# Values ahead of transposes in the prompt attention, and a new order at both ends of the first stage

## The chip, the cores and the metric

One core of one Trainium2 chip. The time is device microseconds of one execution, as the median of several runs. The output must agree with the reference, all of it in float32.

## What is computed

One layer of a hybrid decoder serves a prompt of 1024 tokens and 8 samples of 4 new tokens with 8192 cached ones. Cut to what matters here:

```python
u = rmsnorm(x, attn_pre_g)
qa, kv_a, qi, ki, wi, qb, kb, vb, g_a, g_b = split(u @ w_in)          # rotary on q and k
# branch A: indexer, top 256 keys, softmax attention over these alone
score = sum_h wi[h] * relu(qi[h] . ki);  keep the top 256 admissible keys
o_a = softmax(qa . ka over the kept keys) @ va                          # 8 heads of 64, 2 groups
# branch B: differential attention, 4 heads
o_b = rmsnorm((softmax(q1 k1) - lam * softmax(q2 k2)) @ vb) * (1 - lam_init)
h += rmsnorm((sigmoid(g_a) * (o_a @ w_br_a) + sigmoid(g_b) * (o_b @ w_br_b)) @ w_out)
h += rmsnorm(swiglu(rmsnorm(h)));  h += sigmoid(h @ w_ple_gate) * (p @ w_ple_proj)
```

The outputs are h of the prompt and of the samples, and the new keys and values.

## The kernel before

The program is a row of functions, each a block in which the five engines run their own lists of instructions and meet at a barrier at the end: `project` (line 99, 0 to 438 us: projections of prompt and samples, and the samples' top-k search), `prompt_select` (887), `prompt_attend` (1121, 757 to 1025 us), `sample_select` and `sample_attend` (1818), and the tail with the dense products (2370 on).

**`prompt_attend`.** Its work is 64 units, a unit being one tile of 128 queries of one branch with one of four r: for branch A, r is a head of each of the two groups; for branch B, a head with its two maps. `UNITS` puts them in eight groups k of eight, always alternating A and B: group k takes a branch-A tile `A_TILES[k]` out of [0, 7, 1, 6, 2, 5, 3, 4] and the branch-B tile that mirrors it. A tile i has i + 1 blocks of 128 keys, so each pair has nine blocks in all; groups 0, 2, 4 and 6 have the larger unit in branch B (8, 7, 6 and 5 blocks), groups 1, 3, 5 and 7 in branch A. A unit u passes these steps, by line:

- TensorE, `scores` (1209): products into the two banks `s_bank`, of which there is one pair, so that the scores of u wait until both masks of u - 1 are done (`masked`).
- VectorE, `mask` (1368): adds the bias or the causal mask, and takes the row's extreme (`att_shift`). It moves the scores out of PSUM into `att_masked`, by m = 0 and 1, one CUSTOM_DVE instruction each.
- ScalarE, `exps` (1281): the two exponentials, m = 0 and 1.
- VectorE, `mix`: for A a reciprocal of 128x128 (1377); for B a reciprocal (1381), a weight (1383) and the difference of the two maps, `att_diff` (1388).
- TensorE, `transposes` (1225): 128x128 blocks of the probabilities (A) or of the difference (B), in groups of up to 4 into one of two banks `t_bank`. They wait for the exponentials (A) or for `att_diff` (B), and for the copy of the group before the last.
- ScalarE, `copy_group` (1291): each group of transposed blocks out of PSUM into `att_prob_t`.
- TensorE, `values` (1234 for A's scale, 1240 for A, 1243 for B): the products with the values, 2 to a block for A and 2 to a block as the profile counts them for B; they wait for the unit's last copy and for VectorE's reading of the output bank of the unit before the last.
- VectorE, `out` (1397 to 1405): reads the unit's output.

The order on each engine is written by hand, in rounds s. TensorE's round is scores(s), transposes(s - 2), values(s - 3), and, late in the stage, `turn_tile` (1251), which transposes a finished branch-B tile. ScalarE's is first exponential of s - 1, copies of the first two groups of s - 2, second exponential of s - 1, the other copies. VectorE's is mask(s), mix(s - 1), out(s - 3). SyncE only stores tiles, and GpSimd packs weights for the tail (883).

**`project`.** The prompt's tiles are taken one after the other (p = 0 is the samples' tile, the last is NTILE - 1 = 8). A tile has `begin` (transposes of its normed input, 5 groups), five chunks of `w_in`'s columns, each in four parts of 4 products of 512 columns (chunk 2 is short), and `heads` (transposes of queries and keys, 4 groups). In between, the samples' index search runs in `slots`: 64 groups of `dots`, the scores' layout, then 33 rounds of `count` and `update` (a bisection for the 256th score), `rank`, `before` and `bias`. A planner at the head of the function mixes the two lists: each slot has a weight (`BY_GROUP` 1.1, `BY_LAYOUT` 20, ...), each unit a cost (a part of a chunk 1.7, a group of heads 2.0), and `share`, the sum of costs over the sum of weights, is the budget of unit work that each slot is followed by. `late(order)` then gives TensorE's own list, in which parts of chunks are held back behind the work that others wait for; all five engines walk the same order otherwise. The prompt's rotary, the samples' sums and the counts run on VectorE (the count of one bit is line 757, 128x2052 elements; the rotary writes `pr_row`, 683), the squares and roots of the next tile's input on ScalarE (554 to 564), at the slots of the chunks.

SyncE's list is the same order: loads of x and the layer input for the tile after the next (311, issued when a `begin` slot comes), stores of `u_t`, `xp_t` and the new keys and values at the tile's slots, and at `("lay_out", 1)` the stores of the samples' scores to a DRAM buffer, a wait for all of them, and one load of 1024 KB that brings them back as `pr_flat`, laid out for counting:

```python
if slot[1]:
    sp.wait_ge(score_stored, 16 * 16)
    sp.dma_start(flat[:, 0:SPAN], score_rows.rearrange(...)).then_inc(flat_in, 16)
```

SyncE issues its DMAs in this order and into one queue; the loads of `packed` are in a queue of GpSimd's (q0).

## Time and profile before

| | us |
|---|---|
| median of 3 runs | 3039.74 (3036.61 to 3046.61) |
| the profiled execution | 3034.05 |
| its span | 3032.5 |
| TensorE busy | 2814.4 |
| VectorE busy | 1399.8 |
| GpSimd busy | 676.8 |
| ScalarE busy | 588.0 |

By stage the busy times of TensorE are 386.5 of 438 us (`project`), 315.2 of 319 (`prompt_select`), 229.6 of 268 (`prompt_attend`) and 1883 of 2007.5 (the rest); its granted clock is 0.97 to 0.99 of full in each. The profiled execution's time lies 1.5 us over its span, which is what stands around the first and last instruction. In the profile "PE" is TensorE, "PEld" its weight loads, "DVE" VectorE, "ACT" ScalarE, "POOL" GpSimd and "SP" SyncE; a bracket at the end of an instruction's row gives the time that its engine was idle before it and whose result ended that.

### The profile page before, as it was taken

To read this page: it belongs to the slowest core of one execution; us is meant where nothing else is said; L and a number is where in the kernel's file an instruction comes from. 1 tells how busy PE (TensorE), PEld (TensorE's weight loads), DVE (VectorE), ACT (ScalarE), POOL (GpSimd) and SP (SyncE) were. 2 spreads that over 40 slices of the span, in tenths; PEclk is the share of its full clock that TensorE was granted. 3 is DMA by queue.
4 is the path that set the end of the run, shared out by engine and by line. 5 is a ranking of instruction groups with operands and counts; after the bars stand their busy time and mean duration, and the time that the engine had idled before them with its cause. 6 is when DMAs were issued, how large, how long until landed. Compare 5 with 4: busy or idle time off the path is not lost.

```text
span 3032.5 us, 69638 instructions
## 1 busy us (share of the span) xinstructions
PE 2814.4 (93%) x27060; PEld 1985.4 (65%) x27060; DVE 1399.8 (46%) x2685; ACT 588.0 (19%) x1285; POOL 676.8 (22%) x1190
## 2 busy tenths in 40 slices
PE   7998979999888789999998899999889899999998
PEld 5774544666566567666766667666666666777898
DVE  2337868996678544433344443343434532102211
ACT  2441112001566310101011110011111201001101
POOL 1131003000300001134333333333424334340000
PEclk9999989999999999999999999999999999999999
DMA  7575339521600677799899998889999997673686
GB/s 229 162 203 189 90 122 324 173 71 57 216 8 12 196 223 252 267 306 342 296 338 312 322 331 288 306 297 307 311 324 326 308 311 244 215 230 122 216 268 198
DMA packets 411396, 706.03 MB, mean 233 GB/s; under 512 B 69217, under 2 KB 226017, under 8 KB 410946
## 3 DMA queue, kind: packets, MB, share of 16 engines
q1 hardware_dynamic: 325298, 467.93, 47.0%
q0 software_dynamic: 75456, 232.86, 22.8%
q8 instruction: 215, 3.52, 0.5%
q10 hardware_dynamic: 10320, 0.84, 0.3%
q14 instruction: 107, 0.88, 0.1%
HBM read 659.40 MB, written 90.00 MB: 247 GB/s over the span
## 4 chain that ended last, share of the span: by engine, by line
PE 52%; DMA 4%; issue 3%; DVE 2%; SPq 2%; ACT 2%; DVEq 1%; POOLq 1%; POOL 0%; ACTq 0%
PE sa_t L1685 39%; PE sa_s L2041 4%; PE sa_o L2104 3%; DMA sa_ring_va<-cache_a_kv 2%; PE sa_s L2051 1%; DMA tw_w<-packed 1%; PE sa_stat L2081 1%; DMA early_w<-packed 1%; PE sa_o L2108 1%; ACT sa_prob_t L2182 1%; DVEq L1768 1%; SPq L1996 1%; POOLq L1982 1%; DVE tw_rstd L1760 1%; SPq L1995 0%
## 5 line engine op out<-in xcount | busy, mean ns | idle before, releaser
L1983 POOL DMA_DIRECT2D sa_ring_v<-cache_b_kv x512 | 275.4, 538 | 1097.0 <-PE sa_o L2108 753.3
L2221 DVE STREAM_TRANSPOSE sa_key_b<-sa_ring_k 128x2048 f32<-128x2048 f32 x128 | 295.0, 2307 | 261.6 <-PE sa_s L2041 217.7
L1685 PE MATMUL sa_t<-tw_z,early_w 128*128 128x304 f32 (+1 forms) x1664 | 392.4, 391 | 2.3 <-DVE tw_z L1771 1.4
L1685 PE MATMUL sa_t<-tw_z,tw_w 128*128 128x304 f32 (+1 forms) x1664 | 393.4, 392 | 0.8 <-DVE tw_sig L1774 0.8
L1685 PEld LDWEIGHTS sa_t<-tw_z,early_w 128*128 128x128 f32 x1664 | 285.8, 191 | 93.3 <-issue 19.6
L1685 PEld LDWEIGHTS sa_t<-tw_z,tw_w 128*128 128x128 f32 x1664 | 285.7, 191 | 90.6 <-issue 16.0
L1984 POOL DMA_DIRECT2D sa_ring_va<-cache_a_kv x512 | 274.4, 536 | 53.9 <-issue 27.4
L485 PE MATMUL pr_acc<-pr_w,pr_u_t 128*128 128x512 f32 (+1 forms) x640 | 255.6, 544 | 0.0
L1012 PE MATMUL sel_g<-sel_u,sel_gw 128*128 128x352 f32 x768 | 227.5, 459 | 0.0
L1012 PEld LDWEIGHTS sel_g<-sel_u,sel_gw 128*128 128x128 f32 x768 | 145.8, 190 | 81.9 <-issue 0.8
L2041 PE MATMUL sa_s<-sa_key_b,sa_q_pad 32*32 32x256 f32 x8192 | 183.6, 398 | 4.0 <-issue 4.0
L485 PEld LDWEIGHTS pr_acc<-pr_w,pr_u_t 128*128 128x128 f32 x640 | 109.6, 194 | 94.2 <-issue 94.1
L2104 PE MATMUL sa_o<-sa_ring_v,sa_prob_t 128*8 128x128 f32 x4096 | 139.0, 277 | 25.1 <-DMA sa_ring_va<-cache_a_kv 24.6
L2041 PEld LDWEIGHTS sa_s<-sa_key_b,sa_q_pad 32*32 32x32 f32 x8192 | 119.2, 105 | 56.2 <-issue 26.3
L2104 PEld LDWEIGHTS sa_o<-sa_ring_v,sa_prob_t 128*8 128x8 f32 x4096 | 100.2, 90 | 77.5 <-issue 46.0
L1720 ACT ACTIVATE tw_sig<-sa_t 128x304 f32<-128x304 f32 (+1 forms) x88 | 34.4, 391 | 559.9 <-PE sa_t L1685 559.9
L1685 PE MATMUL sa_t<-early_o,early_w 128*128 128x304 f32 (+1 forms) x512 | 126.1, 400 | 12.5 <-DMA early_w<-packed 4.7
L1701 ACT ACTIVATE tw_sq<-sa_t 128x304 f32<-128x304 f32 (+1 forms) x64 | 25.0, 391 | 511.9 <-PE sa_t L1685 511.9
L1774 DVE TENSOR_TENSOR tw_sig<-sa_t,tw_sig 128x304 f32<-128x304 f32 (+1 forms) x88 | 37.4, 425 | 183.9 <-ACT tw_sig L1720 183.4
L1685 PE MATMUL sa_t<-early_o,tw_w 128*128 128x304 f32 (+1 forms) x512 | 120.7, 390 | 0.8 <-DMA tw_w<-packed 0.7
L1685 PEld LDWEIGHTS sa_t<-early_o,early_w 128*128 128x128 f32 x512 | 89.6, 195 | 41.2 <-issue 16.3
L1685 PE MATMUL sa_t<-tw_x,tw_w 128*128 128x304 f32 (+1 forms) x448 | 106.7, 392 | 1.0 <-DMA tw_w<-packed 1.0
(347 smaller groups left out, 3758.4 us busy)
## 6 DMA issues: line engine op xcount, KB each, us to landing
sa_ring_k<-cache_b_kv SPq DMA_DIRECT2D x512, 256.0 KB, 5.7
sa_ring_v<-cache_b_kv POOLq DMA_DIRECT2D x512, 256.0 KB, 6.2
early_w<-packed SPq DMA_DIRECT2D x168, 512.0 KB, 5.2
tw_w<-packed SPq DMA_DIRECT2D x168, 512.0 KB, 5.9
sa_ring_ka<-cache_a_kv SPq DMA_DIRECT2D x512, 64.0 KB, 5.8
sa_ring_va<-cache_a_kv POOLq DMA_DIRECT2D x512, 64.0 KB, 6.1
packed<-w_gate_up POOLq DMA_DIRECT2D x44, 512.0 KB, 14.7
gate_t<-sel_gate SPq DMA_DIRECT2D x16, 528.0 KB, 3.0
```

Of the source, the lines that this page charges most:

```text
L485: ins = pe.matmul(acc[m % ACC][:, 0:hi - lo], u_t[:, p % 2, k, :], w[:, k, lo:hi], start=(k == 0), stop=(k == KC - 1))
L1012: ins = pe.matmul(g_bank[n % 4][:, 0:PIECE], gw[j % GATE_W][:, k, :], u[:, k, c * PIECE:(c + 1) * PIECE], start=(k == 0), stop=(k == KC - 1))
L1685: ins = pe.matmul(out, self.w[at % self.SLOTS][:, first + k - lo, :], src[:, cols], start=(k == 0), stop=(k == depth - 1))
L1720: nc.scalar.activation(self.sig[:, n % 2, cols], read, ACT.Sigmoid).then_inc(self.sig_set, 1)
L1760: nc.vector.reciprocal(rstd, rstd)
L1768: dve.drain()
L1774: nc.vector.tensor_tensor(sig[:, n % 2], bank, sig[:, n % 2], ALU.mult).then_inc(self.freed_by(g), 1)
L1983: pool.dma_start(ring_v[:, n % RING, :], rows_of(cache_b, page, 1)).then_inc(v_in[n // 4 % 2], 16)
L1984: pool.dma_start(ring_va[:, n % RING, :], rows_of(cache_a, page, 1)).then_inc(va_in[n // 4 % 2], 16)
L2041: ins = pe.matmul(s_bank[32 * h:32 * h + 32, k, 0:CH * 32], q_pad[rows, d, h, 24 - 8 * j:56 - 8 * j], key_b[rows, :, 4 * h + d, :], start= ...
L2104: pe.matmul(o_bank[32 * h:32 * h + 8, 0:P], prob_t[:, g, 0, at:at + 8], ring_v[:, g, h * P:(h + 1) * P], start=False, stop=False, tile_pos ...
L2221: nc.vector.transpose(key_b[:, at:at + 4].rearrange("p g n s -> p (g n s)"), ring_k[:, at:at + 4, :].rearrange("p g e -> p (g e)")).then_i ...
```

## The change

The diff makes two independent edits.

In `prompt_attend`, TensorE's round becomes scores(s), values(s - 3), transposes(s - 2). Nothing else in that function changes.

In `project`, the load of `pr_flat` with its wait becomes a slot of its own, `("lay_in",)`, behind `("lay_out", 1)`. The layout's weight of 20 is split into 8 for the store and 12 for the load, so that the planner puts units between them; the weight of the bias goes from 16 to 22, and `share` falls from 0.854 to 0.836. In the last tile, the group of heads 1 goes from behind chunk 3 to behind chunk 4. By the planner's code, this is what it comes to:

- SyncE: the load of x (512 KB) and of the layer input (128 KB) for tile 5, the store of `u_t` (512 KB) and the store of `xp_t` (640 KB) stand ahead of the wait and of the load of `pr_flat`, and stood behind them.
- TensorE: count 0 stands ahead of the four groups of heads of tile 3, and stood behind them. At the end, the sum of the last count stands ahead of chunk 8 1 2, and stood behind chunk 8 2 0 (chunk p c part); the second group of heads of tile 8 goes behind chunk 8 4.
- VectorE and ScalarE follow the same order; the counts in between are grouped slightly otherwise among the same units.

```diff
--- before.py
+++ after.py
@@ -114,7 +114,7 @@
     chunks = [(0, 512), (512, 1024), (1024, 1092), (1092, 1604), (1604, 2116)]
     pair_cols = [C_QA + P * j for j in range(4)] + [C_KA] + [C_QI, C_QI + P] + [C_KI] + \
                 [C_QB + P * j for j in range(4)] + [C_KB + P * j for j in range(4)]
-    BY_GROUP, BY_LAYOUT, BY_COUNT, BY_RANK, BY_BIAS = 1.1, 20.0, 5.2, 6.0, 16.0
+    BY_GROUP, BY_STORE, BY_LOAD, BY_COUNT, BY_RANK, BY_BIAS = 1.1, 8.0, 12.0, 5.2, 6.0, 22.0
 
     def begin(p):
         return [[("begin", p, g) for g in range(5)]] if p < NTILE else []
@@ -141,16 +141,16 @@
     for p in range(2, NTILE - 1):
         units += chunk(p, 0) + turn_heads(p - 1) + chunk(p, 1) + chunk(p, 2) + chunk(p, 3) + begin(p + 1) + chunk(p, 4)
     last = [[slot] for slot in turn_heads(NTILE - 1)[0]]
-    units += chunk(NTILE - 1, 0) + turn_heads(NTILE - 2) + chunk(NTILE - 1, 1) + chunk(NTILE - 1, 2) + last[0:1] + chunk(NTILE - 1, 3) + last[1:2]
-    units += chunk(NTILE - 1, 4) + last[2:4]
+    units += chunk(NTILE - 1, 0) + turn_heads(NTILE - 2) + chunk(NTILE - 1, 1) + chunk(NTILE - 1, 2) + last[0:1] + chunk(NTILE - 1, 3)
+    units += chunk(NTILE - 1, 4) + last[1:4]
 
     slots = [("small",), ("turn", 0)]
     for n in range(GROUPS):
         slots += [("turn", n + 1)] if n + 1 < GROUPS else []
         slots += [("dots", n)] + {11: [("new_store",)], 27: [("new_load",)], 53: [("lay_out", 0)]}.get(n, [])
-    slots += [("lay_out", 1)]
+    slots += [("lay_out", 1), ("lay_in",)]
     slots += [(kind, i) for i in range(COUNTS) for kind in ("count", "update")] + [("rank",), ("before",), ("bias",)]
-    weights = {"dots": BY_GROUP, "lay_out": BY_LAYOUT, "count": BY_COUNT, "rank": BY_RANK, "bias": BY_BIAS}
+    weights = {"dots": BY_GROUP, "lay_out": BY_STORE, "lay_in": BY_LOAD, "count": BY_COUNT, "rank": BY_RANK, "bias": BY_BIAS}
     share = sum(cost_of(u) for u in units) / sum(weights.get(s[0], 0.0) for s in slots if s != ("lay_out", 0))
     order, budget, spent, g = [s for u in first for s in u], 0.0, 0.0, 0
     for slot in slots:
@@ -415,9 +415,9 @@
                             at = c * 64 + s * 16
                             sp.dma_start(score_rows[s, c, lo * NQ:hi * NQ].rearrange("q p s -> p q s"),
                                          score[at:at + 16, lo * NQ:hi * NQ, :]).then_inc(score_stored, 16)
-                    if slot[1]:
-                        sp.wait_ge(score_stored, 16 * 16)
-                        sp.dma_start(flat[:, 0:SPAN], score_rows.rearrange("j c q p s -> (j c q) (p s)")).then_inc(flat_in, 16)
+                elif slot[0] == "lay_in":
+                    sp.wait_ge(score_stored, 16 * 16)
+                    sp.dma_start(flat[:, 0:SPAN], score_rows.rearrange("j c q p s -> (j c q) (p s)")).then_inc(flat_in, 16)
                 elif slot[0] == "bias":
                     sp.wait_ge(bias_ready, 1)
                     sp.dma_start(a["new_bias"].rearrange("c q s -> (c q) s"), hit[(SLICES - 1) * QS:P, SPAN:FLAT]).then_inc(nb_stored, 16)
@@ -1256,10 +1256,10 @@
                         scores(s)
                     if s < 2:
                         repeat_product(pe, t_bank[0][:, 0, :], ident[:], (3, 9)[s])
+                    if s >= 3:
+                        values(s - 3)
                     if 2 <= s < U + 2:
                         transposes(s - 2)
-                    if s >= 3:
-                        values(s - 3)
                     if 0 <= s - ROOT - 1 < LAST:
                         turn_tile(s - ROOT - 1)
                 repeat_product(pe, s_bank[0][:, 0:P], ident[:], 10)
```

## Rows read from the trace of the kernel before


**Rows 1.** Busy time by engine: PE, PEld, DVE, ACT, POOL; then clock, DMA share, GB/s

```profile
757.00:1025.00 268.00, 229.63 (x1820) 162.06 (x1821) 201.19 (x582) 168.69 (x415) 29.37 (x37) 0.97 0.26 80
```

**Rows 2.** The chain that ended last, prompt attention's end: start, us, what

```profile
1024.83 0.26 SPq L2006
```

**Rows 3.** Waits in the prompt attention: total us, times, longest

```profile
ACT att_prob_t L1291 <- PE att_t L1225: 79.9, 56, 2.8
...
PE att_t L1225 <- DVE att_diff L1388: 11.3, 15, 1.3
...
PE att_t L1225 <- ACT att_prob_t L1291: 9.5, 16, 2.2
```

**Rows 4.** Timeline, first group: start, us, engine, instruction [idle before <- releaser]

```profile
780.70 0.49 PE L1209 MATMUL att_s<-keep_ka,keep_qa 64*128 64x128 f32 x4 [1.28 <-DVE att_shift L1368]
...
781.12 0.44 PE L1225 MATMUL att_t<-keep_ident,att_prob 128*128 128x128 f32 x2
...
781.39 1.95 PE L1243 MATMUL att_o<-keep_vb,att_prob_t 128*128 128x128 f32 x16
...
781.54 0.43 ACT L1291 COPY att_prob_t<-att_t 128x128 f32<-128x128 f32 x2 [0.47 <-PE att_t L1225]
...
781.86 1.16 ACT L1281 ACTIVATE att_prob<-att_masked,att_shift 128x1024 f32<-128x1024 f32 x1
...
783.14 0.17 DVE L1381 RECIPROCAL att_inverse<-att_total 128x2 f32<-128x2 f32 x1 [0.64 <-ACT att_prob L1281]
...
785.67 1.23 DVE L1368 CUSTOM_DVE_ANT_0 att_masked<-att_s,keep_causal 128x1024 f32<-128x1024 f32 x1
...
788.11 1.99 PE L1209 MATMUL att_s<-keep_ka,keep_qa 64*128 64x512 f32 x8 [1.23 <-DVE att_shift L1368]
```

**Rows 5.** Timeline of TensorE, groups 2 and 6 of the prompt attention

```profile
844.61 0.70 PE L1209 MATMUL att_s<-keep_ka,keep_qa 64*128 64x256 f32 x4 [0.97 <-DVE att_shift L1368]
...
845.74 1.73 PE L1243 MATMUL att_o<-keep_vb,att_prob_t 128*128 128x128 f32 x14
...
967.06 1.28 PE L1243 MATMUL att_o<-keep_vb,att_prob_t 128*128 128x128 f32 x10
```

**Rows 6.** Timeline, second group, the large unit in branch A

```profile
811.26 0.49 PE L1209 MATMUL att_s<-keep_kb,keep_qb 64*128 64x128 f32 x4
...
819.09 0.49 PE L1209 MATMUL att_s<-keep_kb,keep_qb 64*128 64x128 f32 x4
...
820.09 0.39 PE L1234 MATMUL att_o<-keep_ident,att_inverse_of 128*128 128x128 f32 x2
...
822.04 0.95 DVE L1377 RECIPROCAL att_inverse_of<-att_total 128x128 f32<-128x128 f32 x1 [0.96 <-ACT att_prob L1281]
...
822.31 0.70 PE L1209 MATMUL att_s<-keep_ka,keep_qa 64*128 64x256 f32 x4
...
823.43 0.42 DVE L1368 CUSTOM_DVE_ANT_0 att_masked<-att_s,keep_bias 128x256 f32<-128x256 f32 x1
```

**Rows 7.** First stage: timelines, DMA share in 0.75 us slices (216:246), issue, busy times

```profile
220.38 13.90 PE L485 MATMUL pr_acc<-pr_w,pr_u_t 128*128 128x512 f32 x32
...
231.31 0.36 SPq L311 DMA_DIRECT2D pr_x<-x_all  x1
...
236.14 2.35 DVE L757 TENSOR_SCALAR_CACHE_REDUCE pr_hit<-pr_flat,pr_edge 128x2052 f32<-128x2052 f32 x1 [6.41 <-DMA pr_flat<-score_rows]
...
240.83 1.94 PE L447 MATMUL pr_turn<-pr_ident,pr_row 128*128 128x128 f32 x8 [5.68 <-ACT pr_heads L564]
...
DMA  9999999999998632100009799999999999999999
...
xp_t<-pr_xp_t SPq DMA_DIRECT2D x1, 640.0 KB, 30.4
...
240.00:246.00 6.00, 5.17 (x14) 3.52 (x15) 2.73 (x5) 2.45 (x8) 3.23 (x4) 0.52 1.06 338
...
420.07 1.11 PE L447 MATMUL pr_turn<-pr_ident,pr_row 128*128 128x128 f32 x4 [8.06 <-DVE pr_row L683]
```

## The prediction

> **What bounds the kernel now.** I read the busy times by stage first, then the chain of waits, then the timelines of the two stages that the diff touches. The program has four stretches between barriers of all engines: the first stage, the prompt's selection, the prompt attention (757 to 1025 us) [rows 1], and the rest. The chain that ended last begins at 1024.8, at the first instruction behind the barrier that closes the prompt attention [rows 2]. So what the first stage or the prompt attention gains or loses moves the end by the same amount; nothing later absorbs it.
>
> In the prompt attention TensorE is the busiest engine (229.6 of 268 us), but it is not full, and neither is VectorE (201) or ScalarE (169). ScalarE waits 79.9 us for TensorE's transposes, in 56 waits; TensorE waits 11.3 us for VectorE's `att_diff` and 9.5 us for ScalarE's copies [rows 3]. Such a picture is a ring of dependences, and the question is which instructions are in the ring.
>
> The timeline shows one pair of units in the first group of tiles, a small unit of branch A (1 block) and a large one of branch B (8 blocks) [rows 4]. Each row starts when the one before it in the ring ends. VectorE ends masking the large unit; TensorE, which had waited 1.28 us for that, makes the small scores at 780.70 and the small transposes at 781.12; ScalarE, which had waited 0.47 us for them, copies at 781.54 and only then runs the second exponential of the large unit, at 781.86 (line 1281 stands behind line 1291 in its order); VectorE waited 0.64 us for it, starts the reciprocal at 783.14, then the mix, and masks the next large unit from 785.67 to 788.0; TensorE's next scores start at 788.11. The period is 788.11 - 780.70 = 7.41 us, and every piece of it is in the ring. The 16 products of the large unit's values (781.39, 1.95 us) are **outside** it: they run after the transposes, beside ScalarE's and VectorE's work.
>
> **The change, prompt attention.** The swap puts those values between the scores and the transposes. The transposes then start one block of values later, so do the copy, the second exponential, the mix, the mask and the next scores. ScalarE's 0.47 us is a wait for these very transposes, so it is no slack. For this group a pair costs 7.41 + 1.88 = 9.3 us (1.95 us less the overlap of the last product). By the same reading the large branch-B units of the other groups put in 14 products in 1.73 us, 12 (between the two), and 10 in 1.28 us [rows 5], so 1.6, 1.4 and 1.2 us; there too the ring has no slack, as TensorE itself waits for the mask ahead of the small scores (0.97 us in the first of them).
>
> With a large unit of branch A the round is bound by TensorE instead, and the ring has room [rows 6]: small scores at 819.09, as soon as the mask is done, scale and values from 820.09 to the next scores at 822.31 (2.22 us), reciprocal at 822.04, next mask at 823.43. The ring is 4.3 us up to that mask, plus two masks of 1024 columns (785.67 to 788.0 [rows 4], 2.3 us) = 6.6, against a period of 7.8. With 2.2 us put in, less 0.35 us for which the small transposes now wait for `att_diff`, it is 8.5, against a period that the same work made 7.8: some 0.8 us more a pair. The same sum gives 0.9, 0.8 and 0.2 us for the other three such groups.
>
> There are 4 pairs in each of the 8 groups: 4 x (1.88 + 1.6 + 1.4 + 1.2) = 24.3 and 4 x (0.8 + 0.9 + 0.8 + 0.2) = 10.8, together 35 us. At the seven borders between groups two large or two small units meet, where I count half of it; that takes about 5 us off. The waits of TensorE for `att_diff` do go, since the values fill them, but TensorE is then in front of a later wait for the mask. I take **+30 us**. Bounds: below, only the branch-B groups pay, for three of their four pairs each and at 2/3: +12; above, all of the 35 and a lower clock (below): +50.
>
> **The change, first stage.** With the new weights and list the planner's code gives this order. What SyncE issues: x and the layer input of tile 5 (640 KB), then the stores of `u_t` (512 KB) and `xp_t` (640 KB), now go ahead of the wait for the stored scores and of the 1024 KB load of `flat`. What TensorE runs: count 0 now stands ahead of the four groups of heads of tile 3, where it stood behind them.
>
> The stall that this aims at is plain: TensorE ended tile 4's first chunk at 234.28, did two groups of transposes and then waited 5.68 us, until 240.83, for ScalarE [rows 7], which sat in front of the square of tile 5's x; that load was issued only behind `flat`, at 231.31. With x issued some 9 us earlier this wait goes. Next is what is late then: TensorE reaches count 0 at 234.3, and count 0 needs `flat`, which landed at 236.14, plus 2.35 us of counting, so TensorE stands until some 238.9 (236.14 + 2.35, and the rest of the count, estimated at 0.4; 4.6 us), and only then makes 16 transposes, of which it made 8 before. By 243 it has done the same work as before. The swap of waits alone is worth nothing, 0 us.
>
> `flat` itself is issued behind 1.8 MB of the same queue. The spread: at the 338 GB/s of the stretch behind it [rows 7] these are 5.3 us, of which the idle time of the DMA engines from 228.7 to 231 (slices 18 to 20 of rows 7's line of 40) may hide some or nothing; the `xp_t` store took 30.4 us to land when GpSimd's packing was in flight, which would make `flat` some 20 us late. I take +4, near the former: most of the stores' way lies in the idle time, and the packing resumes only at 232. The ends are 0 and +20, and the latter is a rival below. Behind the waiting count on VectorE stand the rotary of tile 4's first chunk and all other counts; TensorE waits for them.
>
> After the transposes of the heads the clock matters: from 240 to 246 us TensorE had a granted clock of 0.52, its level of 1.2 GHz, after the stall, and 8 transposes took 1.94 us [rows 7]. I take the same cost for either order. The Trainium skill, TensorE: Matmul & The Clock Gate, Part 4: PE-mode transpose, says that transposes do not count as busy time for the clock; by that the clock would come back only behind the products that follow, and the first stage would lose some 1.5 us more, since twice the transposes now come first. The rows fit either reading.
>
> At the end of the stage the work goes the other way. TensorE waited 8.06 us at 420.07 for the rotary of the last tile's second chunk, which VectorE does behind the bias [rows 7]. Now the last count stands earlier in TensorE's list: two parts of chunk 1 and one of the short chunk 2 of the last tile lie behind it instead of ahead (8 instructions of 13.90 / 32 = 0.43 us [rows 7] and 4 short ones, some 4 us) and fill the wait, and the heads that waited go behind chunk 4. I take -5; the bounds are 0 and the wait itself, -8. The counts between hold the same work on both engines in another grouping: 0, from -2 to +3, one count of 2.35 us out of step either way.
>
> **Sum.** Profiled execution 3034.05 us, + 30 + 4 - 5 = 3063. That execution lies 5.7 us below the median of the three runs, 3039.74; on the median's scale the forecast is 3069 us. About 0.3% (9 us) is what a measurement of this kernel tells from no change.
>
> **The rivals.**
> (1) TensorE is the bound, and filling its waits pays. Then its 11.3 us for `att_diff` and some of the 9.5 us for copies go, and with -1 of the first stage the time is 3039.74 - 17 = 3023. This needs ScalarE's second exponential to have slack behind the small transposes. It decides the sign: the ring must have more than the block's 1.2 to 2.2 us to spare; [rows 4] show none, [rows 6] show 1.1. Chance 0.07. [...]
> (2) The clock. With the longer rounds TensorE's share falls from 86% to 77%; at 86% the granted clock of the stage was 0.97 [rows 1], so it fell now and then. If a third of the stage were at the low level, the small scores and the block in the ring would cost twice as much: about +15 more, 3084. Chance 0.14.
> (3) `flat` is stuck behind the stores: +16 beyond the 4, 3085. Chance 0.06.
> (4) The rings overlap and half of the loss is absorbed: +15 in place of +30, 3054. Chance 0.11.
> (5) The loss is small and meets the gain of the first stage's end: 3042. Chance 0.05; that the order does not change is excluded, as the lists differ.
> The forecast itself has 0.57, and its own range is 3059 to 3079. The range 3047 to 3091 takes in (2), (3), (4) and the bounds, and leaves (1) and (5) out. Slower by over 0.3%: 0.57 + 0.14 + 0.06 + 0.11 = 0.88; within: 0.05; faster: 0.07.
>
> **What would show it.** In the profile after: the prompt attention is near 298 us where it was 268; in its first pairs the scores of small units are 9.3 us apart; TensorE's wait for `att_diff` falls below 3 us while its wait for `att_shift` (the mask) grows to some 30 or more, and ScalarE's for transposes grows beyond 100. In the first stage: the 5.68 us wait is gone and one of about 5 to 9 us stands ahead of count 0, with `flat` landing 0 to 8 us later; the 8.06 us wait shrinks to 4 or less. The prediction is wrong if the second exponential of a large unit does not start later against the mask before it.

## The result, and the profile after

The changed kernel takes 3069.77 us (median of 4 executions, 3065.26 to 3072.98); the kernel before, timed beside it, 3038.35 us. The ratio is 1.0105, with a 95% interval of 1.009 to 1.0121: the change makes the kernel about 31 us slower. The forecast was 3069 us, with a range of 3047 to 3091.

The busy times by stage of the kernel after (columns as in [rows 1]; the borders are this kernel's own barriers):

```profile
0.00:434.00 434.00, 387.10 (x2053) 245.23 (x2055) 236.92 (x515) 114.00 (x256) 60.92 (x77) 0.98 0.54 163
...
753.50:1053.90 300.40, 243.54 (x1820) 166.51 (x1820) 200.71 (x581) 168.64 (x415) 29.20 (x36) 0.96 0.24 72
1053.90:3068.90 2015.00, 1890.57 (x22197) 1399.78 (x22197) 694.32 (x910) 255.24 (x514) 550.67 (x1029) 0.97 0.83 279
```

The first stage ends at 433.8 us where it ended at 438.4. The prompt attention, 753.5 to 1053.9, takes 300.4 us where the kernel before took 266.9 (757.9 to 1024.8, both from TensorE's first scores to the first load behind the barrier) [rows 2], with the same instructions in it: VectorE is busy for 200.7 us and ScalarE for 168.6, as before, and TensorE for 243.5 where it was 229.6. The rest takes 2015.0 us against 2007.7. That last difference is not the change's: over the profiles of all the kernels below, none of which differs there, the rest takes between 2002.9 and 2017.6 us. So between the two profiled executions (3070.48 and 3034.05 us) the sum is -4.6 + 33.5 + 7.3, plus 0.2 in the stage between, and between the medians some 31.

The waits in the prompt attention, of the kernel after, over the whole of that stage (total us, times, longest; the kernel before's, over its whole stage, are those of [rows 3]):

```profile
ACT att_prob_t L1291 <- PE att_t L1225: 117.9, 60, 5.5
...
DVE att_inverse L1381 <- ACT att_prob L1281: 35.8, 22, 3.8
...
PE att_s L1209 <- DVE att_shift L1368: 29.7, 30, 1.9
...
PE att_t L1225 <- DVE att_diff L1388: 8.9, 11, 2.2
```

ScalarE's wait for transposes grew from 79.9 to 117.9 us and TensorE's wait for the mask (`att_shift`), which was 10.3 us, to 29.7. TensorE's wait for `att_diff` fell from 11.3 to 8.9 only. VectorE now waits 35.8 us for the second exponential ahead of the reciprocal, from 16.8.

One pair of units in the first group, timeline of the kernel after, which answers to [rows 4]:

```profile
767.64 0.49 PE L1209 MATMUL att_s<-keep_ka,keep_qa 64*128 64x128 f32 x4 [1.20 <-DVE att_shift L1368]
...
768.06 2.05 PE L1243 MATMUL att_o<-keep_vb,att_prob_t 128*128 128x128 f32 x16
...
769.95 0.38 PE L1225 MATMUL att_t<-keep_ident,att_prob 128*128 128x128 f32 x2
...
770.31 0.43 ACT L1291 COPY att_prob_t<-att_t 128x128 f32<-128x128 f32 x2 [1.68 <-PE att_t L1225]
770.63 1.16 ACT L1281 ACTIVATE att_prob<-att_masked,att_shift 128x1024 f32<-128x1024 f32 x1
...
771.91 0.17 DVE L1381 RECIPROCAL att_inverse<-att_total 128x2 f32<-128x2 f32 x1 [2.42 <-ACT att_prob L1281]
...
774.44 1.23 DVE L1368 CUSTOM_DVE_ANT_0 att_masked<-att_s,keep_causal 128x1024 f32<-128x1024 f32 x1
...
776.88 0.49 PE L1209 MATMUL att_s<-keep_ka,keep_qa 64*128 64x128 f32 x4 [1.94 <-DVE att_shift L1368]
```

The rows are the ring, in its order: small scores at 767.64, now the 16 products of the large unit's values for 2.05 us, and only then the two small transposes at 769.95; ScalarE waited 1.68 us for them (0.47 before), copies, and starts the second exponential at 770.63, 2.99 us behind the scores where it was 1.16 us behind (780.70 to 781.86 in [rows 4]); VectorE waited 2.42 us for it (0.64), masks from 774.44, and TensorE's next scores start at 776.88, 9.24 us after the last ones. Before it was 7.41.

The first stage, timeline of the kernel after, which answers to [rows 7]:

```profile
217.33 13.90 PE L485 MATMUL pr_acc<-pr_w,pr_u_t 128*128 128x512 f32 x32
...
218.82 0.36 SPq L311 DMA_DIRECT2D pr_x<-x_all  x1
...
225.11 1.62 SPq L420 DMA_DIRECT2D pr_flat<-score_rows  x1
...
234.43 2.35 DVE L757 TENSOR_SCALAR_CACHE_REDUCE pr_hit<-pr_flat,pr_edge 128x2052 f32<-128x2052 f32 x1 [7.75 <-DMA pr_flat<-score_rows]
...
237.07 0.59 PE L543 MATMUL pr_once<-pr_count,pr_same 128*128 128x1 f32 x2 [5.85 <-DVE pr_flipped L759]
...
237.52 3.91 PE L447 MATMUL pr_turn<-pr_ident,pr_row 128*128 128x128 f32 x16
...
413.89 9.87 PE L485 MATMUL pr_acc<-pr_w,pr_u_t 128*128 128x512 f32 x16 [3.69 <-DVE pr_row L683]
```

The 5.68 us wait for ScalarE is gone, and one of 5.85 us ahead of the sum of count 0 (L543) stands in its place. All 16 transposes of the heads come behind it. At the end, the wait for the last tile's rotary has shrunk from 8.06 to 3.69 us; it now stands ahead of products (L485), as the heads that waited have moved behind them.

### The profile page after: what moved, and what is told of

Read it like the earlier page. It is cut to its first block, busy times and chain, and to the rows that moved or that the text cites. A ratio compares the mean times of both kernels' runs of the same rounds, so it can differ in the third digit from the quotient of the medians.

```text
span 3068.9 us, 69638 instructions
## 1 busy us (share of the span) xinstructions
PE 2836.5 (92%) x27060; PEld 1995.9 (65%) x27060; DVE 1399.4 (46%) x2685; ACT 587.4 (19%) x1285; POOL 676.4 (22%) x1190
## 4 chain that ended last, share of the span: by engine, by line
PE 52%; DMA 4%; issue 3%; DVE 2%; ACT 2%; SPq 1%; POOLq 1%; DVEq 1%; POOL 0%; ACTq 0%
PE sa_t L1685 39%; PE sa_s L2041 4%; PE sa_o L2104 4%; DMA sa_ring_va<-cache_a_kv 2%; PE sa_s L2051 1%; PE sa_stat L2081 1%; DMA tw_w<-packed 1%; PE sa_o L2108 1%; ACT sa_prob_t L2182 1%; DMA early_w<-packed 1%; POOLq L1982 1%; PE sa_t L1655 1%; DVE tw_rstd L1760 0%; DVEq L1768 0%; DMA y<-tw_y_row 0%
## 5 line engine op out<-in xcount | busy, mean ns | idle before, releaser
L485 PE MATMUL pr_acc<-pr_w,pr_u_t 128*128 128x512 f32 (+1 forms) x640 | 254.4, 543 | 3.7 <-DVE pr_row L683 3.7
L485 PEld LDWEIGHTS pr_acc<-pr_w,pr_u_t 128*128 128x128 f32 x640 | 109.0, 194 | 97.9 <-issue 93.3
L1685 PE MATMUL sa_t<-early_o,early_w 128*128 128x304 f32 (+1 forms) x512 | 123.4, 394 | 11.8 <-DMA early_w<-packed 6.0
L1685 PEld LDWEIGHTS sa_t<-early_o,tw_w 128*128 128x128 f32 x512 | 87.5, 190 | 30.2 <-issue 7.6
```

The lines of the kernel that those rows point to most:

```text
L485: ins = pe.matmul(acc[m % ACC][:, 0:hi - lo], u_t[:, p % 2, k, :], w[:, k, lo:hi], start=(k == 0), stop=(k == KC - 1))
L1685: ins = pe.matmul(out, self.w[at % self.SLOTS][:, first + k - lo, :], src[:, cols], start=(k == 0), stop=(k == depth - 1))
```

## Experiments

All times are beside runs of the kernel before on the same chip. "Pair" is the time from one reciprocal of a branch-A unit (line 1377 of the kernel before) to the next, one pair of units; "attention" is from the first scores to the first load behind the barrier, and "first stage" the start of the next stage's first product, each of the profiled execution.

| kernel | ratio to before (95%) | first stage ends | attention |
|---|---|---|---|
| before | 1 | 438.4 | 266.9 |
| after | 1.0105 (1.009 to 1.0121) | 433.8 | 300.4 |
| attn_only | 1.0138 (1.012 to 1.0156) | 436.2 | 303.1 |
| first_only | 0.9986 (0.9977 to 0.9995) | 433.8 | 267.0 |
| exps_after | 0.998 (0.9967 to 0.9993) | 436.4 | 261.6 |
| exps_before | 0.9964 (0.995 to 0.9977) | 437.4 | 256.8 |
| swap_large_turn | 1.0019 (1.0009 to 1.003) | 439.7 | 269.7 |
| swap_small_turn | 1.0132 (1.0115 to 1.0149) | 438.5 | 303.4 |
| exps_first | 0.996 (0.9946 to 0.9974) | 432.5 | 256.9 |
| exps_large | 0.9956 (0.9941 to 0.997) | 438.4 | 254.4 |
| exps_large_ahead | 0.9958 (0.9939 to 0.9976) | 439.6 | 252.9 |
| exps_large_first | 0.9945 (0.9928 to 0.9962) | 436.5 | 254.8 |
| first_load | 0.9994 (0.9979 to 1.0008) | 443.0 | 265.4 |
| first_end | 0.9966 (0.995 to 0.9983) | 432.7 | 263.2 |

**The two edits apart.** attn_only is the kernel before with

```diff
-                    if 2 <= s < U + 2:
-                        transposes(s - 2)
                     if s >= 3:
                         values(s - 3)
+                    if 2 <= s < U + 2:
+                        transposes(s - 2)
```

> Only the swap in the prompt attention, the first stage as before. Theory (a ring of scores, transposes, copy, second exponential, mix and mask takes in the values): the prompt attention takes 300 us as in the changed kernel, 33.5 us more than before, and the whole 3072 us. Rival (part of the loss of the whole change comes from the first stage, through when transfers and packing reach the attention): the attention takes 285 us or less, the whole under 3060.

Measured: the attention takes 303.1 us, the whole 3074.65 against 3036.55. The loss belongs to the swap alone; the rival falls.

first_only is the changed kernel with that swap taken back.

> Only the new order of the first stage, the attention as before. In the changed kernel the first stage is 4.6 us shorter, of which 3.0 us were already there before the stored scores are loaded, where only a stall of 2.6 us near 184 us is missing. If the gain is the end of the stage alone: 3038.4 - 2 to - 4, some 3035 us. If the missing stall belongs to the new order too: 3038.4 - 5, some 3033 us. If the stage after the attention, which took 7.3 us longer in the changed kernel's profile, is slower because of the first stage: 3040 us or more.

Measured: 3031.74 against 3036.55 us, a gain of 4 us give or take 3. The attention's pairs are those of the kernel before (7.41 and 7.42 us in the first group), so the first stage's new order does not reach them. The rest of this profiled execution took 2017.6 us, the longest of all; but the 11 timed runs lie lower (this profile's 3039.5 is their highest), so that rest is no part of the change.

**The ring cut on ScalarE.** exps_after is the changed kernel, and exps_before the kernel before, with

```diff
                     if s - 1 < U:
                         exps(s - 1, 0)
+                        exps(s - 1, 1)
                     if 2 <= s < U + 2:
                         for g in range(min(2, len(groups[s - 2]))):
                             copy_group(s - 2, g)
-                    if s - 1 < U:
-                        exps(s - 1, 1)
```

> The changed kernel, with both exponentials of a unit ahead of the copies on ScalarE instead of the copies of the first two groups between them. Theory (the values delay the small transposes, these the copy, and the copy the second exponential, which stands behind it in ScalarE's list): the ring is cut there, the attention falls from 300 to some 275 us, the whole to 3045. Rival (the loss comes from the lower granted clock in the attention, or from TensorE having too much to do): the cut changes little, attention 295 us or more, the whole 3063 or more.

> The kernel before, with both exponentials of a unit ahead of the copies. Theory: the ring is shorter by the small copy (0.32 us) and ScalarE's wait (0.47 us) in the groups whose large unit is in branch B, and the copies of large units come later, which TensorE's transposes into two banks wait for: attention 262 to 270 us (267 before), the whole 3034 to 3042. Rival (the copies are what TensorE needs first): attention above 275, the whole above 3047.

Measured: exps_after 3029.68 us, attention 261.6; exps_before 3023.33 us, attention 256.8. Nothing was changed on TensorE, and 39 us of attention went between the changed kernel and exps_after, 10 us between the kernel before and exps_before. The same pair as above, timeline of exps_after (its lines behind 1281 stand one line higher):

```profile
776.84 0.49 PE L1209 MATMUL att_s<-keep_ka,keep_qa 64*128 64x128 f32 x4 [0.79 <-DVE att_shift L1367]
...
777.26 2.05 PE L1243 MATMUL att_o<-keep_vb,att_prob_t 128*128 128x128 f32 x16
...
777.80 1.15 ACT L1281 ACTIVATE att_prob<-att_masked,att_shift 128x1024 f32<-128x1024 f32 x1
...
779.15 0.38 PE L1225 MATMUL att_t<-keep_ident,att_prob 128*128 128x128 f32 x2
...
779.51 0.43 ACT L1291 COPY att_prob_t<-att_t 128x128 f32<-128x128 f32 x2 [0.47 <-PE att_t L1225]
...
781.62 1.23 DVE L1367 CUSTOM_DVE_ANT_0 att_masked<-att_s,keep_causal 128x1024 f32<-128x1024 f32 x1
...
784.05 1.13 PE L1209 MATMUL att_s<-keep_ka,keep_qa 64*128 64x512 f32 x4 [0.79 <-DVE att_shift L1367]
```

The values still stand ahead of the small transposes, the copy is still late at 779.51, but the second exponential already starts at 777.80, as soon as the first ends; the next scores come 7.21 us after these. With TensorE's old order (exps_before) the pair is 7.17: in this pair the swap costs 0.04 us where it costs 1.8 with the ring closed. Over the whole attention it still costs 4.8 us (261.6 against 256.8), so the loss is gone but for a seventh; 1.3 us of the rest stand in the first pair behind the first group (9.34 against 8.04), and where the others come from was not followed up. Both forecasts were too careful: the theory said 275 and 262 to 270 us. The ring had bound the kernel before as well. Its waits in exps_before say so (total us, times, longest):

```profile
ACT att_prob_t L1291 <- PE att_t L1225: 64.4, 61, 3.4
...
PE att_s L1209 <- DVE att_shift L1367: 8.5, 16, 1.0
...
DVE att_inverse L1380 <- ACT att_prob L1281: 1.0, 1, 1.0
```

VectorE's wait for the exponential ahead of the reciprocal (L1380 here) is 1.0 us, where it was 16.8.

**Which half of the swap.** swap_large_turn and swap_small_turn are the kernel before with the swap in half of the rounds:

```diff
+                    ahead = s >= 3 and (s - 2 >= U or blocks_of(s - 2) > blocks_of(s - 3))
+                    if ahead:
+                        values(s - 3)
                     if 2 <= s < U + 2:
                         transposes(s - 2)
-                    if s >= 3:
+                    if s >= 3 and not ahead:
                         values(s - 3)
```

and with `<` for `>` in the second.

> The kernel before, with the values ahead of the transposes only in the rounds where the unit to be transposed is the larger of the two, so that a small unit's values (0.8 to 1.5 us) go ahead of a large unit's transposes. Theory: the copy of a large unit is not what its neighbour's second exponential waits for, and these transposes stood waiting for the difference anyway, so the small values fill that wait: attention 263 to 268 us (267 before), the whole 3033 to 3038. Rival (any values ahead of any transposes cost their own length): these hold about 3 tenths of the swapped products, attention 275 to 278 us, the whole 3046.

> The complement: the values ahead of the transposes only in the rounds where the unit to be transposed is the smaller, so that a large unit's values (1.3 to 2.2 us) go ahead of a small unit's transposes. Theory: this half holds the whole loss, attention 299 to 304 us, the whole 3070 to 3075. Rival (each swapped block costs its own length): attention 290 to 293 us, the whole 3061.

Measured: with a small unit's values ahead of a large unit's transposes, attention 269.7 us and the whole 0.2% slower; with a large unit's values ahead of a small unit's transposes, 303.4 us and 1.3% slower. The second half holds the whole loss and the rival falls, since it had put 3 tenths on the other. The first half was not as harmless as I expected: +2.8 us, not -4 to +1, though TensorE's wait for `att_diff` fell from 11.3 to 4.1 us. In the first group its pairs are 7.62 and 7.45 us (7.42 and 7.41 before); in the fourth to the seventh some are longer by 0.5 to 0.7 us (7.84, 8.09, 7.87 and 8.15). Why is open. The whole, 3043.0 us, also missed its forecast of 3033 to 3038. Timeline of TensorE in swap_small_turn, first group:

```profile
773.36 0.49 PE L1209 MATMUL att_s<-keep_ka,keep_qa 64*128 64x128 f32 x4 [0.60 <-DVE att_shift L1371]
...
782.60 0.49 PE L1209 MATMUL att_s<-keep_ka,keep_qa 64*128 64x128 f32 x4 [1.35 <-DVE att_shift L1371]
...
783.02 2.05 PE L1243 MATMUL att_o<-keep_vb,att_prob_t 128*128 128x128 f32 x16
```

The period is 9.24 us, as in the changed kernel (767.64 to 776.88), and so is the next one, where the changed kernel's has 10.60 (see the clock, below).

**The first stage, part by part.** first_load keeps the bias's weight of 16 and the last heads' old place, and takes only the load slot; first_end takes only those two and leaves the layout in one piece:

```diff
first_load
-    BY_GROUP, BY_LAYOUT, BY_COUNT, BY_RANK, BY_BIAS = 1.1, 20.0, 5.2, 6.0, 16.0
+    BY_GROUP, BY_STORE, BY_LOAD, BY_COUNT, BY_RANK, BY_BIAS = 1.1, 8.0, 12.0, 5.2, 6.0, 16.0
...
-    slots += [("lay_out", 1)]
+    slots += [("lay_out", 1), ("lay_in",)]
first_end
-    BY_GROUP, BY_LAYOUT, BY_COUNT, BY_RANK, BY_BIAS = 1.1, 20.0, 5.2, 6.0, 16.0
+    BY_GROUP, BY_LAYOUT, BY_COUNT, BY_RANK, BY_BIAS = 1.1, 20.0, 5.2, 6.0, 22.0
...
-    ... + chunk(NTILE - 1, 3) + last[1:2]
-    units += chunk(NTILE - 1, 4) + last[2:4]
+    ... + chunk(NTILE - 1, 3)
+    units += chunk(NTILE - 1, 4) + last[1:4]
```

> The kernel before with only the layout split into a store and a load slot (weights 8 and 12), the bias's weight and the last heads as before. Theory (this part exchanges TensorE's wait for the square of tile 5's x against one for count 0, and delays the load a little): from the transposes of tile 5's x to the end of the four groups of heads 25.5 us where the old order takes 23.6 (mean of three profiles), the wait of 8.06 us near 420 stays, the first stage ends some 2 us later, the whole +2 us. Rival (removing the 5 us wait pays by itself): the stage ends 2 us or more earlier.

> The complement: the bias's weight 22 and the last heads' new place, the layout in one slot as before. Theory: the wait ahead of the last tile's heads shrinks from 8.06 to some 3.7 us, and the 1.69 us wait near 186 us goes, as these come from the weight and not from the load's place: the first stage ends 4 to 5 us earlier, at 432 to 434 us, the whole -4 us. Rival (they come from the load's place): both waits stay.

Measured: first_load 0.9994, no difference that counts; first_end 0.9966, that is 10 us faster, with an interval of 5 to 15. In its profile the first stage ends 5.7 us earlier, and the attention, whose code is that of the kernel before, is 3.7 us shorter, most of it by the clock (see below); what of the 10 us is the change's is open. Timelines of first_load and of first_end:

```profile
233.08 1.97 SPq L420 DMA_DIRECT2D pr_flat<-score_rows  x1
...
245.25 0.59 PE L543 MATMUL pr_once<-pr_count,pr_same 128*128 128x1 f32 x2 [5.38 <-DVE pr_flipped L759]
...
424.51 1.12 PE L447 MATMUL pr_turn<-pr_ident,pr_row 128*128 128x128 f32 x4 [8.06 <-DVE pr_row L683]
```

```profile
227.60 0.34 SPq L420 DMA_DIRECT2D pr_flat<-score_rows  x1
...
232.73 2.35 DVE L757 TENSOR_SCALAR_CACHE_REDUCE pr_hit<-pr_flat,pr_edge 128x2052 f32<-128x2052 f32 x1 [3.43 <-DMA pr_flat<-score_rows]
...
235.37 0.38 PE L543 MATMUL pr_once<-pr_count,pr_same 128*128 128x1 f32 x2 [1.53 <-DVE pr_flipped L759]
...
238.46 1.94 PE L447 MATMUL pr_turn<-pr_ident,pr_row 128*128 128x128 f32 x8 [1.77 <-ACT pr_heads L564]
...
413.11 9.92 PE L485 MATMUL pr_acc<-pr_w,pr_u_t 128*128 128x512 f32 x16 [3.69 <-DVE pr_row L683]
```

The gain of the first stage belongs to first_end, whose wait near 413 us is 3.69 us and which has none of the 1.69 us wait near 186 that the old weights have in all eight profiles. The early wait can only come from the bias's weight, since the last heads stand 200 us behind it; which of the two shrinks the late one was not separated. first_load keeps the 8.06 us wait. There I was wrong in a detail: in first_load TensorE's heads still stand ahead of count 0, so it is the weight of the bias, through `share`, that moves count 0 ahead of them, and not the load's slot (the planner's code gives the same order). Nor was the path as long as forecast: from the transposes of tile 5's x to the first product behind the heads and count 0 it is 23.9 us, where I had said 25.5, and 21.9 us in first_end. In first_end `flat` is issued ahead of x, lands 5.1 us later (227.60 to 232.73), and the two waits that follow are 1.53 and 1.77 us. With the load slot as well (the changed kernel) `flat` takes 9.3 us (225.11 to 234.43), and the wait is 5.85. From TensorE's transposes of tile 5's x to the end of the stage it is 218.7 us in the mean of seven profiles of the old order, 216.6 in five of the whole new one, 221.2 in first_load and 214.5 in first_end. By the means the load slot costs 2 to 2.5 us and the rest gains 4. But the five profiles of the new order fall into two kinds, 213.8 and 213.9 us against 218.1 to 218.9, and the clock parts them. The 16 products behind the 3.69 us wait take 7.13 us in the first two and 9.75 to 9.96 us in the other three, and in first_end. Timeline of first_only, to be held against the last rows of the two timelines of the kernel after and of first_end:

```profile
416.80 7.13 PE L485 MATMUL pr_acc<-pr_w,pr_u_t 128*128 128x512 f32 x16 [3.70 <-DVE pr_row L683]
```

At the same clock there, the load slot costs 3.9 us (218.4 against 214.5). With one profile of first_end and one of first_load, 2 to 4 us is as close as it can be put.

**Versions that beat both.** exps_first adds the new first stage to exps_before; exps_large adds to exps_before the half of the swap that had cost little (small values ahead of large transposes); exps_large_first has all three; exps_large_ahead is the kernel before with the second exponential ahead only where its unit is the larger one:

```diff
+                    ahead = s - 1 < U and s >= 2 and blocks_of(s - 1) > blocks_of(s - 2)
                     if s - 1 < U:
                         exps(s - 1, 0)
+                    if ahead:
+                        exps(s - 1, 1)
                     if 2 <= s < U + 2:
                         for g in range(min(2, len(groups[s - 2]))):
                             copy_group(s - 2, g)
-                    if s - 1 < U:
+                    if s - 1 < U and not ahead:
                         exps(s - 1, 1)
```

> TensorE's order of the attention as before, both exponentials ahead of the copies on ScalarE, and the new first stage: the two that gained alone. Additive: 3023 - 4 = 3019 us, the attention at 257. Rival (the gains overlap, or the rest of the program takes the first stage's gain back): 3023 or more.

> Both exponentials ahead of the copies, the first stage as before, and the small units' values ahead of the large units' transposes. With the ring cut TensorE (230 us busy of 257) is nearer to being what bounds, so filling its waits for the difference (some 6 us) could pay: attention 252 to 257 us, the whole 3019 to 3023. Rival (the large transposes and their copies now end the round, so the small values ahead of them cost their length in part): attention 260 to 264 us, the whole 3027 to 3031.

> The kernel before, with the second exponential ahead of the copies only where the unit of the exponential is the larger one; where it is the smaller, the large unit's copies go first as before. Theory: the gain comes from the ring's large exponential alone, so the groups with the large unit in branch B have pairs of 7.17, 6.9, 6.6 and 6.4 us as with both ahead, and in the others TensorE's transposes get their banks back sooner (8.1 and 7.8 us in group 1 in place of 8.8 and 7.8): attention 254 us, the whole 3021. Rival (the large unit's copies ahead put a new wait into the ring): attention 259 us or more.

> Both exponentials ahead, the small units' values ahead of the large units' transposes, and the new first stage. Additive from the profiles: attention 254.4, first stage 4 us shorter: some 3018 us. Rival (the first stage's gain is within the spread of the rest of the program): 3020 to 3023.

Measured: 3022.4, 3021.91, 3025.58 and 3021.85 us, all 0.4 to 0.55% under the kernel before, and not to be told from one another, nor from exps_before alone (0.9964). By the profile, exps_large_ahead has the shortest attention (252.9 us; forecast 254): its large-B pairs are those of exps_before, 7.16 and 6.89 us, so the large unit's exponential alone was the ring's link. That TensorE would get its banks back sooner in the second group is not confirmed: the first of those two pairs is 8.86 us, not 8.1. Its whole, 3025.58, missed the 3021 of the forecast. exps_large's 254.4 us is as forecast, though exps_before's wait for the difference, which it was to fill, is 3.6 us and not some 6. exps_large_first's 3021.85 us is the rival's value (3020 to 3023), not the theory's 3018. Of the first stage's gain hardly a part shows in exps_first's time (0.9960 against exps_before's 0.9964, 0.9 us between the medians; the forecast was 4), within the spread of the rest of the program. The likely best, exps_large_ahead with first_end's first stage, was not run.

## Why the prediction was right, and where its terms were off

**The bound.** That nothing later absorbs a change of either stage: right, the 33.5 us of the attention and the -4.6 us of the first stage both arrive at the end.

**The ring.** Its mechanism is right, and shown from two sides: moving the values of large units alone gives the whole loss, and taking the second exponential out from behind the copy takes all but 4.8 us of it away with TensorE's order unchanged. The price of an ordinary pair is right too. The third pair of each group (in the first and the third group the second, as the third lost clock), after less before: first group 9.21 - 7.42 = 1.8 (forecast 1.88), third 8.88 - 7.44 = 1.4 (1.6), fifth 8.84 - 7.47 = 1.4 (1.4), seventh 8.66 - 7.49 = 1.2 (1.2); branch A large: 8.42 - 7.82 = 0.6 (0.8), 8.26 - 7.37 = 0.9 (0.9), 8.09 - 7.37 = 0.7 (0.8), and 9.35 - 8.39 = 1.0 (0.2).

**How many pairs pay.** This is the step that was off. I had all four pairs of a branch-B group pay in full. But the first pair of each costs nothing (6.65 us against 6.66 before, 7.18 against 7.44, 7.45 against 7.60, 7.73 against 7.81), and in the fifth and the seventh group the second costs 0.6 and 0.3 us only (8.06 and 7.76 us). In swap_small_turn the same two are 8.84 and 8.65, so it takes the other half of the swap to make them short; how is open. The three pairs inside each branch-B group, 18.2 us in my sum, brought 11.8 in all, and those inside the branch-A groups 5.1 (5.4 in my sum).

**The borders.** Here the term was mis-sized, and with the wrong sign. I took off 5 us, as if each border cost half a pair. At the borders from a group with the large unit in B to one with it in A, two large units meet, and the last pair and the first cost together 12.47 + 10.69 - 9.51 - 8.65 = 5.0 us, and 5.1, 3.2 and 4.5 at the other three, 17.7 in all and half of the loss; at the other borders the last pair is 0.2 to 0.6 us longer. All the pairs come to 35.7 us, and the attention to 33.5, as its start and end are 2.2 us shorter. That my +30 came so near is in good part luck: too many pairs at full price, and borders that I had put at less than nothing.

**A sign that did not come.** TensorE's wait for `att_diff` was to fall below 3 us, as the values fill it, and is 8.9. In the pair of [rows 4] its matmuls had not waited for the difference at all, and in the same pair of the changed kernel it waits 0.81 us: the difference hangs on the second exponential, so it is late with the ring. The other signs came: 9.24 us between the small scores (9.3), 29.7 us for the mask (30 or more), 117.9 us for transposes (beyond 100), the attention at 300.4 us (298).

**The clock**, rival (2), came true in a small part. It is in the attention's granted clock, 0.96 where it was 0.97, and in single pairs. Busy times of the kernel after (columns as in [rows 1]):

```profile
775.00:780.00 5.00, 3.12 (x19) 3.01 (x20) 3.61 (x11) 2.18 (x6) 0.00 (x0) 0.78 1.00 302
853.00:857.00 4.00, 4.00 (x19) 2.78 (x17) 0.55 (x4) 2.16 (x6) 0.00 (x0) 0.58 0.01 2
```

and TensorE's values in the first of these stretches:

```profile
777.30 3.31 PE L1243 MATMUL att_o<-keep_vb,att_prob_t 128*128 128x128 f32 x16
```

The 16 products take 3.31 us, where those of the pair before took 2.05: TensorE had waited 0.81 us for the difference and 1.94 us for the mask, and the clock fell to its level of 1.2 GHz for a part of them. In the ring such a block costs the round its added length: the third pair of the first group is 10.60 us, and 9.24 in swap_small_turn, whose granted clock was 1.00 there. That is 1 to 2 us a time, in a few places that differ from profile to profile (11.38 us for the same pair in attn_only). +15 us it was not: granted clocks of 0.96 and 0.97 are, with two levels, some 24 and 16 us at the lower one, and 8 us more at half the speed cost some 4 us at most (an estimate from these two figures). The kernel before has them too: the first pair of the second group is 8.65 us there and 7.07 in first_end, the second of the last group 11.01 and 9.43 (granted clocks 0.93 and 0.85 against 1.00 in both), which is most of the difference between the attention's 266.9 and 263.2 us in these two.

**TensorE as the bound**, rival (1), is refuted for these two orders. Its waits for `att_diff` were partly filled, and that cost 33.5 us; an edit on ScalarE, the least busy of the three, gained 10 us of attention. The Trainium skill, Perfetto Trace Analysis, Identifying the Most-Contended Engine, says that the engine with the highest occupancy is to be optimized first, and that TensorE is not to be judged by the busy share of its matmuls but, among other things, by that of its weight loads. By matmuls TensorE leads here (229.6 of 268 us), by weight loads (162.1, the second number of [rows 1]) it stands behind VectorE (201.2). The traces agree with neither as the place to work: what paid was the order on ScalarE, at 168.7 us.

**The first stage.** The forecast was -1 from +4 and -5, and a waits' exchange worth 0; the profile gave -4.6, and the mean of profiles (434.6 in five with the new order, 438.3 in seven with the old) -3.7. The exchange was right: 5.68 us gone, 5.85 come. `flat`'s load took 9.3 us in place of 5.3, which is the +4 as forecast, but the path from the transposes of tile 5's x to the first product behind heads and count lost only 2.3 us of it (25.5 against 23.2 us in the mean). The end gained 4.4 us of the wait (8.06 to 3.69), for which I had taken 5. From tile 5's x on, the part that I had compared, the profile gave -1.6 us and the means -2.1, with -1 forecast. What I missed lies ahead of it: a 1.69 us wait near 186 us for the copy of a key's transposes goes with the new weights. I had compared the two orders from the layout on, and not the groups of `dots` ahead of it, whose units the lower `share` moves as well.

The size of the +4 was right, its reason only in part. I had reckoned with the transfers of SyncE's own queue, and with GpSimd's packing only from 232 us on. GpSimd's DMA queue while `flat` was under way (packets, MB, share of the 16 DMA engines' time), in the kernel before (230.84 to 236.14) and in the kernel after (225.11 to 234.43):

```profile
q0 software_dynamic: 1, 0.00, 0.0%
```

```profile
q0 software_dynamic: 348, 1.30, 40.6%
```

So the load met 1.3 MB of packing beside the stores that stood ahead of it, and no run here tells the two apart.

**The sum** was right partly because errors met. In the attention the pairs' count was too high and the borders too low, which left 3.5 us too little, and the first stage was some 3 us too high.

## What to carry to other kernels

Before you fill a busy engine's waits, follow one round from a mask to the next and write down which instructions release one another; here a block put into that ring cost nearly its whole length (1.8 of 1.95 us), and blocks moved beside it cost little (2.8 us for all of them), on the busiest engine of the stage. Then count how many rounds are of that kind, and look at the rounds where one kind gives way to another by themselves: half of the loss was there. Where a long instruction stands behind a short copy in one engine's list although it does not need it, the order of that engine is the lever: here exponentials moved ahead of copies gained 10 us of the attention, and the whole new order of the first stage 4. A planner's weight moves everything behind and ahead of the step that it was meant for, so compare the two orders from the first difference on.

## What the runs showed of the hardware

After a wait, the clock could come back while TensorE made transposes. In exps_first TensorE had waited 5.33 us, then made two short products, the 16 transposes of the heads, and only then long products. Timeline of TensorE, and busy times by 1 us (columns as in [rows 1]):

```profile
239.54 0.58 PE L543 MATMUL pr_once<-pr_count,pr_same 128*128 128x1 f32 x2 [5.33 <-DVE pr_flipped L759]
239.99 3.61 PE L447 MATMUL pr_turn<-pr_ident,pr_row 128*128 128x128 f32 x16
243.44 1.88 PE L485 MATMUL pr_acc<-pr_w,pr_u_t 128*128 128x512 f32 x4
```

```profile
242.00:243.00 1.00, 1.00 (x5) 0.81 (x6) 1.00 (x2) 0.66 (x3) 0.00 (x0) 0.50 1.03 252
243.00:244.00 1.00, 1.00 (x6) 0.76 (x6) 0.78 (x5) 0.95 (x2) 0.00 (x0) 0.92 1.04 240
244.00:245.00 1.00, 1.00 (x4) 0.44 (x3) 0.93 (x3) 0.22 (x1) 0.00 (x0) 1.00 0.96 361
```

The granted clock is 0.50 up to 243 us and 0.92 in the next microsecond. With two levels that is some 0.16 us at 1.2 GHz and then 2.4 GHz, so it rose at about 243.2, ahead of the first long product at 243.44, which with three others took 1.88 us. In first_only it rose likewise, at about 244.4, 0.1 us ahead of the product at 244.45. In the other three profiles of the new order it rose 0.3 to 1.1 us behind the first long product. The prediction gave what the Trainium skill (TensorE: Matmul & The Clock Gate, Part 4: PE-mode transpose) says, that transposes do not count as busy time, and the 1.5 us that it would cost. By that rule the clock should have stayed low until long products came, unless the two of 128x1 (0.58 us) ahead of the transposes were enough; these two traces do not agree with it, and the other three fit it.

A load of 1024 KB took 5.3 us from its issue to the start of what waited for it with no transfer ahead of it and GpSimd's queue idle, and 9.3 us when 1.8 MB of other transfers of the same queue stood ahead of it and GpSimd's queue took 40.6% of the DMA engines' time.
